# Layer norms in two parts, placed among the second's output tiles, and a final norm applied to transposed outputs

## The reference, cut to what matters

```python
def rms_norm(x, g):
    y = x * lax.rsqrt(jnp.mean(x * x, axis=-1, keepdims=True) + EPS)
    return y * g

# each layer of either block
h = rms_norm(x, norm_g[l]) * (1 + scale) + shift     # scale, shift, gate from a small product of c
p = h @ w_in[l]                                       # split into the branches
...
x = x + gate * (y @ w_out[l])
# behind the last layer
return rms_norm(x, final_g)
```

## Time and profile before

| what | us |
|---|---|
| median of 3 runs (3356.74 to 3358.87) | 3356.97 |
| the profiled execution, its own time | 3351.97 |
| its span in the profile | 3350.0 |
| PE busy, with share of the span | 3178.7 (95%) |
| DVE busy | 1321.2 (39%) |
| ACT busy | 837.8 (25%) |
| POOL busy | 1601.5 (48%) |

### The profile page before, as it was taken

One profiled execution on the slowest core, in us unless ns is written; L12 is line 12 of the kernel. 1 busy time (PEld: TensorE's weight loads), 2 busy tenths in 40 slices (PEclk: granted clock), 3 DMA queues, 4 the chain that ended last, 5 costly groups with the idle time before them and its releaser, 6 DMA issues.

```text
span 3350.0 us, 40006 instructions
## 1 busy us (share of the span) xinstructions
PE 3178.7 (95%) x14939; PEld 2286.2 (68%) x14939; DVE 1321.2 (39%) x2508; ACT 837.8 (25%) x1522; POOL 1601.5 (48%) x1507
## 2 busy tenths in 40 slices
PE   7999997999999999998989999999999999999988
PEld 4666665656666555465778758888984588889944
DVE  3021346545554412326666543434332334343322
ACT  4123225421111122325411112332110123321110
POOL 1788996000000059961444237875640287766500
PEclk9999998999999999998999999999999999999999
DMA  6111110024443121110234322222221222222211
GB/s 227 42 38 32 38 36 4 13 76 126 130 141 120 41 63 38 44 38 1 80 113 142 99 76 65 75 76 63 76 76 51 65 76 64 76 67 72 76 50 38
DMA packets 259330, 236.58 MB, mean 71 GB/s; under 512 B 20886, under 2 KB 257346, under 8 KB 259140
## 3 DMA queue, kind: packets, MB, share of 16 engines
q1 hardware_dynamic: 259140, 234.02, 23.0%
HBM read 231.91 MB, written 2.10 MB: 70 GB/s over the span
## 4 chain that ended last, share of the span: by engine, by line
PE 82%; DVE 8%; POOL 5%; ACT 2%; issue 2%; DMA 1%; DVEq 0%; ACTq 0%; POOLq 0%; SPq 0%
PE ps L470 30%; PE ps L1175 21%; PE ps L500 10%; PE ps L1017 5%; PE ps L1219 2%; DVE arena L1797 2%; POOL arena L2430 2%; DVE small L2015 2%; PE ps L757 2%; ACT arena L1312 1%; PE ps L486 1%; PE ps L1263 1%; DVE bQz L1801 1%; PE ps L1121 1%; POOL arena L2429 1%
## 5 line engine op out<-in xcount | busy, mean ns | idle before, releaser
L2430 POOL TENSOR_TENSOR arena<-arena,posi 128x512 f32<-128x512 f32 (+1 forms) x360 | 409.7, 1138 | 30.0
L470 PE MATMUL ps<-hT,wring 128*128 128x512 f32 (+1 forms) x1184 | 407.3, 504 | 0.7 <-ACT arena L1312 0.7
L500 PE MATMUL ps<-hT,wring 128*128 128x512 f32 (+1 forms) x1024 | 373.8, 520 | 1.9 <-ACT arena L1312 1.8
L470 PE MATMUL ps<-arena,wring 128*128 128x512 f32 (+1 forms) x992 | 367.9, 531 | 0.0
L470 PEld LDWEIGHTS ps<-hT,wring 128*128 128x128 f32 x1184 | 229.2, 195 | 170.1 <-issue 154.9
L1312 ACT ACTIVATE arena<-ps 128x256 f32<-128x256 f32 (+4 forms) x403 | 176.7, 438 | 667.3 <-PE ps L470 234.7
L2512 POOL TENSOR_TENSOR arena<-wring 128x512 f32<-128x512 f32 x72 | 92.9, 1290 | 460.2 <-PE ps L1175 279.7
L470 PEld LDWEIGHTS ps<-arena,wring 128*128 128x128 f32 x992 | 187.6, 190 | 175.2 <-issue 168.4
L500 PEld LDWEIGHTS ps<-hT,wring 128*128 128x128 f32 x1024 | 192.9, 193 | 153.2 <-issue 144.3
L2429 POOL TENSOR_SCALAR posi<-arena,cols 128x512 f32<-128x512 f32 (+1 forms) x360 | 248.8, 691 | 35.4
L1797 DVE TENSOR_TENSOR arena<-arena 128x768 f32<-128x768 f32 (+7 forms) x120 | 173.4, 1445 | 191.9 <-ACT arena L1312 188.0
(11 more groups left out here) (263 smaller groups left out, 4924.2 us busy)
## 6 DMA issues: line engine op xcount, KB each, us to landing
wring<-in_w_in SPq DMA_DIRECT2D x126, 1024.0 KB, 5.3
wring<-in_w_mod SPq DMA_DIRECT2D x24, 1024.0 KB, 8.2
wring<-in_w_out SPq DMA_DIRECT2D x24, 1024.0 KB, 6.0
wring<-in_w_ada SPq DMA_DIRECT2D x21, 1024.0 KB, 5.2
wring<-in_w_conv_out SPq DMA_DIRECT2D x7, 512.0 KB, 6.2
wring<-in_w_gla_out SPq DMA_DIRECT2D x7, 512.0 KB, 6.2
wring<-in_w_attn_out SPq DMA_DIRECT2D x7, 512.0 KB, 5.5
arena<-in_w_ada SPq DMA_DIRECT2D x3, 1024.0 KB, 5.2
```

Of the source, the lines that this page charges most:

```text
L470: last = eng.matmul(o_(out), a, b_, start=(i == 0), stop=(i == len(parts) - 1))
L500: mm = eng.matmul(bank[b][:, 0:n], w[:, k, j * P:(j + 1) * P], hT[:, k, t0:t0 + n], start=(k == 0), stop=(k == KD - 1))
L2430: pool.link(eng.tensor_tensor(dst, dst, scratch, ALU.add))
```

## The change

The norm between two layers is done in two parts: x and then c for L = 1, the two halves of x ("x0", "x1", 256 tokens each) for L = 2, 3 and 4. The last two output tiles, j = 6 and 7, are computed as four part tiles in the order (6, first), (7, first), (6, second), (7, second). The sum of squares and the spread of the first part are put between steps of the second part's tiles; those of the second part are put between steps of `first_product`. ACT and DVE take their steps in a matching order; `SPLIT` says how many scaled rows of the first part stand ahead of the second part's last residual or root. In the second block the gate product is in two halves, the second one behind the first quarter product, and the first group's products come in another order, each with a wait for its own sum of h.

For the final norm, ACT multiplies the rows of `xT` by the final weight as they come (`weighted`), PE turns them, units 0 and 1 between steps of tile (6, x1), and the norm of a token is applied as a scale per partition in the copies out of PSUM, half by ACT and half by DVE. `xout` moves to another place, and there are eight output DMAs of half a unit. The squares go to `WT` there, since `hT` holds the weighted rows.

PE claims banks 4 and 5 (before: 4) ahead of tile 3 in the second block, and the rings of banks are changed.

```diff
+        SPLIT = {1: 4, 2: 6, 3: KD}
+        def norm_parts(L):
+            return ("x", "c") if L < 2 else ("x0", "x1")
...
+            def last_tiles(L, y, ws, K, src, between):
+                p0, p1 = norm_parts(L)
+                for j, sg in ((6, p0), (7, p0), (6, p1), (7, p1)):
+                    t0, n = SEG[sg]
+                    key = ("y", y, j, sg)
+                    b = next_bank("V", key)
+                    for k in range(K):
+                        for do, *what in between.get((j, sg, k), ()):
+                            do(*what)
+                        mm = eng.matmul(bank[b][:, 0:n], ws[j - 6](k), src(k, t0, n), start=(k == 0), stop=(k == K - 1))
+                    mm.then_inc(*pe.tell(("full", key)))
...
+                    first_product(bank[b][0:32 + RANK, 0:SEG[sg][1]], w, l, sg, 32 + RANK,
+                                  [(2, square_sum, "c"), (5, spread_norms, "c")] if l and sg == "x" else ())\
...
-                square_sum(l + 1)
-                spread_norms(l + 1)
+                last_tiles(l + 1, l, [lambda k: w[:, k, 0:P], lambda k: w[:, k, P:2 * P]], KD,
+                           lambda k, t0, n: mT[:, k, t0:t0 + n],
+                           {(6, p1, 7): [(square_sum, l + 1, p0)], (7, p1, 3): [(spread_norms, l + 1, p0)]})
...
+                gate_half(0, [(3 + l, square_sum, "x1"), (6 + l, spread_norms, "x1")])
...
                     product(bank[x_][:, 0:HALF], quarter[0][0], w[:, 0:4, 0:P], True, turned)
+                    begin = k[1:] == (0, 0)
+                    if begin:
+                        gate_half(1).then_inc(*pe.tell(("full", ("if", l))))
...
+                    if begin:
+                        claim(y_)
+                        eng.wait_ge(*at(("h sum", l, 0)))
+                        product(bank[y_][:, HALF:TX], hsum[0], t1, True, turned)
...
-                claim(4)
-                rings[0] = {"A": [0, 1], "V": [2, 3, 6, 7]}
+                claim(4, 5)
+                rings[0] = {"A": [0, 1], "V": [2, 6, 3, 1]}
...
+                if L == 2:
+                    between = {(6, "x1", 6): [(square_sum, 3, "x0")], (6, "x1", 11): [(spread_norms, 3, "x0")]}
+                else:
+                    between = {(6, "x1", 4): [(turn_output, 0, range(KD))], (6, "x1", 6): [(square_sum, 4, "x0")],
+                               (6, "x1", 9): [(turn_output, 1, range(KD))]}
...
+            turn_output(2, range(KD - 1))
+            square_sum(4, "x1")
+            turn_output(2, [KD - 1])
+            turn_output(3, range(KD))
...
+            def output(u):
+                eng.wait_ge(*at(("inverse", 4, ("x0", "x1")[u // 2])))
+                evac(("final", u, 0), xout[:, u, 0:512], 0, 512, scale=ncol[:, 2 + u:3 + u])
...
+            def layer_end(L, y):
+                for j in (6, 7):
+                    residual(L, y, j, p0)
+                    squares(L, j, p0)
+                inverse(L, p0)
+                if L == 3:
+                    scaled(L, p0, range(KD))
+                if L == 4:
+                    output(0)
+                    output(1)
+                residual(L, y, 6, p1)
+                squares(L, 6, p1)
+                if L < 3:
+                    scaled(L, p0, range(SPLIT[L]))
+                residual(L, y, 7, p1)
+                squares(L, 7, p1)
+                if L < 3:
+                    scaled(L, p0, range(SPLIT[L], 6))
+                inverse(L, p1)
+                if L < 3:
+                    scaled(L, p0, range(6, KD))
+                if L < 4:
+                    scaled(L, p1, range(KD))
+                else:
+                    output(2)
+                    output(3)
...
-                eng.wait_ge(*at(("free", ("final", u, 1))))
-                eng.dma_start(out[0, u * P:(u + 1) * P, :], xout[:, u, :]).then_inc(m.sem("out_done"), 16)
+                for half in range(2):
+                    eng.wait_ge(*at(("free", ("final", u, half))))
+                    part = slice(512 * half, 512 * half + 512)
+                    eng.dma_start(out[0, u * P:(u + 1) * P, part], xout[:, u, part]).then_inc(m.sem("out_done"), 16)
```

More of the change, by code:

```diff
@@ L574, in _ @@
             mod_no = [0, 0]
[L576 to L600, removed]
+            def square_sum(L, sg):
+                t0, n = SEG[sg]
+                i = norm_parts(L).index(sg)
+                claim(4 + i)
+                eng.wait_ge(*at(("squares", L, sg)))
+                if L == 0:
+                    mm = eng.matmul(bank[4 + i][:, 0:n], ones, rstd[:, t0:t0 + n], start=True, stop=True)
+                else:
+                    for u in UNITS[sg]:
+                        mm = eng.matmul(bank[4 + i][:, u:u + 1], rstd[:, u * P:(u + 1) * P], ones[:, 0:1],
+                                        start=True, stop=True)
+                mm.then_inc(*pe.tell(("ss", L, sg)))
@@ new lines, in spread_norms @@
+            def spread_norms(L, sg):
+                b = 4 + norm_parts(L).index(sg)
+                key = ("nbc", L, sg)
+                eng.wait_ge(*at(("inverse", L, sg)))
+                for i, u in enumerate(UNITS[sg]):
+                    mm = eng.matmul(bank[b][:, i * P:(i + 1) * P], ncol[:, u:u + 1].broadcast_to([P, P]), ident,
+                                    start=True, stop=True)
+                mm.then_inc(*pe.tell(("full", key)))
+                bank_of[key], last_on[b] = bank[b], key
@@ new lines, in turn_output @@
+            def turn_output(u, ks):
+                two = (0, 7) if u % 2 == 0 else (1, 2)
+                for k in ks:
+                    b, key = two[k // 4], ("final", u, k // 4)
+                    if k % 4 == 0:
+                        claim(b)
+                    eng.wait_ge(*at(("weighted", ("x0", "x1")[u // 2], k)))
+                    mm = eng.transpose(bank[b][:, k % 4 * P:k % 4 * P + P], hT[:, k, TC + u * P:TC + (u + 1) * P], ident)
+                    if k % 4 == 3:
+                        mm.then_inc(*pe.tell(("full", key)))
+                        bank_of[key], last_on[b] = bank[b], key
@@ L1349, in head_of_layer, with first_head @@
+            def first_head():
+                act.stage("norm")
+                deviation(0, "x")
+                for i in (3, 4, 5):
+                    first_mod(i)
+                deviation(0, "c")
+                for i in (6, 7):
+                    first_mod(i)
+                eng.wait_ge(*at(("first shifts",)))
+                shifted(0, "x", range(KD))
+                shifted(0, "c", range(KD))
             def head_of_layer(L):
                 act.stage("norm")
-                if L:
-                    fn(small[:, 90:91], eps[:, :], ACT.Sqrt)
@@ L1364, in head_of_layer @@
[L1364 to L1371, removed]
+                p0, p1 = norm_parts(L)
+                fn(small[:, 90:91], eps[:, :], ACT.Sqrt)
@@ L1808, in _, with residual @@
             dve.link(eng.memset(cpad, 0.0), ("c clear",))
[L1809 to L1817, removed]
+            def residual(L, y, j, sg):
+                t0, n = SEG[sg]
+                c_ = 1 if sg == "c" else 0
+                k = ("y", y, j, sg)
+                eng.wait_ge(*at(("full", k)))
+                stt(xT[:, j, t0:t0 + n], bank_of[k][:, 0:n], modT[:, (L - 1) % 3, 16 + j, c_:c_ + 1],
+                    xT[:, j, t0:t0 + n], M_, A_, ("free", k))
@@ L2405, in _ @@
                 dve.stage("out2")
-                for j in range(KD):
-                    k = ("y", L, j, "x")
-                    eng.wait_ge(*at(("full", k)))
-                    stt(xT[:, j, TC:T], bank_of[k][:, 0:TX], modT[:, L % 3, 16 + j, 0:1], xT[:, j, TC:T], M_, A_, ("free", k))
-                    squares(L + 1, j)
-            norm(4)
+                for j in range(KD - 2):
+                    residual(L + 1, L, j, "x")
+                    squares(L + 1, j, "x")
+                layer_end(L + 1, L)
         @block.gpsimd
```

238 lines of the change are left out of this document (146 added, 92 removed).

## The result

The median went from 3357.92 us (3356.74 to 3364.08) to 3335.83 (3329.72 to 3345.09): ratio 0.9936, 95% interval 0.9921 to 0.9950. The profiled execution of the changed kernel took 3334.75, its span is 3333.1. So the kernel became 21.5 to 22 us faster; 29.5 were forecast.

What follows compares the result with a forecast made beforehand. It took PE's chain of waits at the four norms between layers, with the low clock there, as the bound. Gains 5.1 + 6.4 + 6.5 + 12.4 - 0.9 = 29.5 off median 3356.97 gave 3327.5 us; range 3321.5 to 3336.5.

Steps and rivals of the forecast that it cites:

- First boundary: Norm done as x, then c: PE walks into the gate product, waiting 0.8 for the sum of c; gain 5.1 us.
- Second: Norm in halves x0, x1 before the first group: PE waits 1.1 for x1's squares; gain 6.4 us, POOL moving along.
- Third: Norm before the second group, tiles of 16 steps: 8.4 us, less 1.4 for the claim and 0.5 for POOL: 6.5.
- Claim: Ahead of tile 3, PE waits for bank 5, held by early tile 2: 1.4 us lost, at third boundary and before tail.
- Tail: Final norm: eight scalings and six of eight copies leave the path; gain 13.8 us, 12.4 after the claim's 1.4.
- Hand-overs: Each of fourteen sums and spreads put into PE's stream costs 0.06 us: 0.9 lost in all.
- What would show it: Signs: PE gaps at most 1.2 us into L486, clock near 1.00, 1.4 us wait before tile 3, first group earlier.
- Rival 1: Second parts run later, DVE 0.95 slower beside POOL in four places, tail transposes at half clock: 6 to 8 lost; chance 0.14.
- Rival 2: Second-block first heads paced by weight landing or earlier POOL work: 6.4 + 6.5 vanish, 3340.4 us; chance 0.08 with rival 4.
- Rival 3: Between the boundaries, 384 matmuls of 256 columns each wait 0.19 for weight loads: 73 us more, 3400; chance 0.03.
- Rival 4: A claim or bank makes PE wait out the first part; at worst tail's 12.4 stands, 3344.6 us; chance 0.08 with rival 2.
- Rival 5: No loss beside POOL, no claim wait, cheaper last DMAs: gain 34.3, time 3322.7 us; chance 0.06.

Runs made afterwards that it cites:

- the experiment: Changed kernel with TensorE claiming bank 4 alone, not banks 4 and 5, ahead of tile 3: 3331.42 us, ratio 0.9921 to the kernel before.
- the tail's edit: Changed kernel with both turned units of x0 and its column sum behind the last tile instead of inside tile (6, x1): 3335.06 us.
- POOL's: Changed kernel with POOL's pair sums for the second group waiting until the squares of x1 are summed: 3334.75 us.
- the sums moved back: Changed kernel with the first part's column sum and spread behind the last tile at the first three boundaries: 3348.39 us, ratio 0.9967 to the kernel before.

## Why the prediction was right, and where its sizes were off

It named the mechanism at the boundaries, and the time lies in its range. That it does is in part luck: the median is 0.7 us inside the range's upper end and 8.3 above the forecast, while single executions run from 3329.72 to 3345.09. By its steps:

- *First boundary:* 5.1 forecast, 5.3 measured. The wait for the sum of c was 0.69 (0.8 forecast).
- *Second:* 6.4 forecast, 5.3 measured. The wait for x1's squares, 1.09, came as forecast (1.1). What was mis-sized is PE's own pace: sums, spreads and changes from one product to the next cost a little each, 1.1 us up to the end of the group.
- *Third:* 8.4 less 0.5 for POOL forecast, 6.5 measured. POOL cost 0.9, as its removal showed; a wait of 0.44 for the first sum of h and the slower pace made up the rest.
- *Claim:* 1.4 twice forecast, 1.7 and 1.05 measured, together as forecast; the experiment confirmed its cause.
- *Tail:* 13.8 forecast, 13.7 measured. That the DMAs cancel was right too. What the single steps of its new form are worth wasn't measured.
- *Hand-overs:* the 0.9 that I had taken stands for some 2.0, all of it in the second and third boundaries, with the wait of 0.44 in it. The sum is 28.0 instead of 29.5.
- *What it left out:* the clock outside the boundaries, which it took to stay as it was. Off the medians the sum would give 3329 to 3330; 3332.7 and 3335.8 came. Over the later 22 executions of before and the five of the changed kernel beside them, the means are 24.7 apart, so 3 us of the 28.0 are missing on average, about what the clock moves a median by. For the second cell the loss is more than scatter. Its second head start ran at full clock in both profiles of before (73.5 us to the next start) and at half clock behind its wait in all seven profiles with the change and no extra matmul (75.2). In the first cell it did so in four of the seven; it kept its clock in the kernels with the tail's edit, with POOL's, and with the sums moved back. Filling the waits brought it back to 73.5 in every profile. Why the shortened boundaries place these waits worse isn't shown.
- *What would show it:* the first group was to be over 5, 11.5 and 18 us earlier in turn. By the windows it was 4.5, 4.7 and 6.6, because the stretches between the boundaries were longer than in the first profile of before: by the claim's wait, by the clock in the cells, and because that one execution was quick in the layer behind the first boundary.

Rival 1 (late second parts) held in one place and cost 0.9, not 6 to 8. Rival 2 (middle gains don't carry) was refuted by moving the sums back. Rival 3 (half-width matmuls bound by weight loads) did not occur: 46 records of 256 columns took 10.09 us in the second boundary's part tiles, 0.219 each, against 0.216 before; 384 records at 0.003 more make 1 us. So the rule of the Trainium skill ("TensorE: Matmul & The Clock Gate", section "Part 3: Packing small matmuls — row/col tiling") that speaks for it isn't borne out here. The same section also lets weights be loaded ahead into a background buffer, which would fit this pace; no run shows which it is. Rival 4 (a claim makes PE wait out the first part) did not occur: inside the part tiles of the timelines PE waits for nothing. Rival 5 (more) fell with the claim's wait and POOL's loss, which both came.

## What to carry to other kernels

Put the small steps of a chain over several engines (sum, root, spread) into the stream of products ahead of it, and split the data so that the first part's chain runs behind the second part's tiles; a scale per row can wait until the outputs are copied. Where TensorE's short gaps lower its clock, compare kernels over several executions with their clocks, because one pair of profiles can hide a third of the gain, as here (16.9 of 28.0 us at first sight, 24.7 in the means). Look too at what a shortened stretch does to the clock behind it. And once such gaps are known, a matmul whose result nobody reads, placed only where TensorE waits anyway, can be worth about half as much as the restructuring.

## What was not expected of the hardware

Behind the waits of about 1.1 us at the second to fourth head starts of a cell, the granted clock stood at 1.2 GHz in 46 of 54 cases (nine profiles of kernels without extra matmuls) and at 2.4 GHz in the other eight. Which it was didn't depend on the length of the wait alone: 1.10 us kept the clock in the first timeline above and 1.07 lost it in the second. With an extra matmul in the wait it stayed at 2.4 GHz in all 30 cases of five profiles. Each fall cost 1.7 us, and the median fell by 13 us or more with eight extra matmuls. The Trainium skill ("TensorE: Matmul & The Clock Gate", section "A second HAM failure mode: psum-queue depth-cycling") tells of a bf16 kernel in which short idle times between groups of matmuls make the clock swing between its levels; these float32 runs agree.
